# Encoder trunk on one core: order of VectorE's and ScalarE's work around the four retention heads

## The reference

```python
def retention_mixer(h, w_in, w_out, pos):
    q, k, v, g = split(h @ w_in, [D, 2*D, 4*D])          # 4 heads: q, k 256 wide, v, g 512 wide
    q = rotary(q, pos); k = rotary(k, pos) * 256 ** -0.5
    # both directions of the chunked form together give
    o = (q @ k.T * gamma_h ** abs(n - m)) @ v
    o = (o - mean(o)) * rsqrt(var(o) + 1e-6)             # per token and head
    return (silu(g) * o) @ w_out

def rglru_one_direction(x, w_a, b_a, w_i, b_i, lam, reverse):
    r = sigmoid(x @ w_a + b_a); i = sigmoid(x @ w_i + b_i)
    log_a = -8.0 * r * softplus(-lam)                    # softplus(-lam): the "rates", 16 columns here
    a = exp(log_a); u = sqrt(-expm1(2.0 * log_a)) * (i * x)
    return scan(a, u)
```

## Time and profile before

| | before |
|---|---|
| median of 3 runs | 721.08 us (720.83 to 721.31) |
| the profiled execution | 720.02 us, span 718.2 us |
| PE busy, PEld busy | 98%, 82% of the span |
| DVE busy, ACT busy, POOL busy | 85%, 72%, 3% |
| mean granted clock of PE | 0.994 |
| moved by DMA | 134.31 MB, 187 GB/s on average |

### The profile page before, as it was taken

The page is one execution under the profiler, slowest core; times in us unless marked ns, Lnnn a source line. Parts: engine busy times, 40 slices in busy tenths (PEclk is TensorE's granted clock), DMA queues, the critical chain, the costliest instruction groups (busy, mean ns, idle before and its releaser), DMA issues.

```text
span 718.2 us, 15923 instructions
## 1 busy us (share of the span) xinstructions
PE 700.4 (98%) x6495; PEld 586.6 (82%) x6495; DVE 611.4 (85%) x828; ACT 518.5 (72%) x834; POOL 24.4 (3%) x26
## 2 busy tenths in 40 slices
PE   9979999999899999999999999999999999999996
PEld 7858888787699888888888999888888888885464
DVE  6967788887869799998899879999999999999643
ACT  7475673938467688787887688899758889888441
POOL 0001001020010000000000300000000000000000
PEclk9989999999999999999999999999999999999999
DMA  9964634445465165555579961020436656665821
GB/s 343 304 245 134 247 123 144 166 127 213 142 241 205 61 211 201 206 201 175 178 260 407 367 256 60 28 93 1 166 117 195 224 197 215 234 210 208 274 42 59
DMA packets 47323, 134.31 MB, mean 187 GB/s; under 512 B 29728, under 2 KB 30240, under 8 KB 32032
## 3 DMA queue, kind: packets, MB, share of 16 engines
q1 hardware_dynamic: 46976, 133.20, 52.7%
q10 hardware_dynamic: 288, 0.31, 0.1%
HBM read 129.17 MB, written 1.05 MB: 181 GB/s over the span
## 4 chain that ended last, share of the span: by engine, by line
PE 81%; DVE 8%; ACT 6%; SPq 2%; issue 2%; DMA 1%; DVEq 0%; ACTq 0%
PE ps L1638 21%; PE ps L1639 21%; PE ps L1640 21%; PE ps L2075 3%; PE ps L2074 3%; PE ps L2073 3%; SPq L479 2%; DVE w_lo L1006 1%; PE ps L1680 1%; PE ps L1685 1%; PE ps L1681 1%; PE ps L1762 1%; PE ps L1758 1%; PE ps L1759 1%; PE ps L2013 1%
## 5 line engine op out<-in xcount | busy, mean ns | idle before, releaser
L1638 PE MATMUL ps<-a_hi,w_hi 128*128 128x272 f16 (+1 forms) x1000 | 278.2, 278 | 6.2 <-DVE mT L1160 6.2
L1640 PE MATMUL ps<-a_hi,w_lo 128*128 128x272 f16 (+1 forms) x1000 | 278.1, 278 | 0.0
L1639 PE MATMUL ps<-a_lo,w_hi 128*128 128x272 f16 (+1 forms) x1000 | 278.1, 278 | 0.0
L1006 DVE SCALAR_TENSOR_TENSOR w_lo<-stage,w_hi 128x1024 f16<-128x1024 f32 x207 | 248.5, 1229 | 30.7 <-ACT w_hi L548 30.4
L548 ACT ACTIVATE w_hi<-stage 128x1024 f16<-128x1024 f32 x207 | 210.3, 1047 | 51.8 <-PE ps L1640 24.2
L1638 PEld LDWEIGHTS ps<-a_hi,w_hi 128*128 128x128 f16 x1000 | 98.3, 98 | 23.5 <-DVE mT L1160 6.8
L1640 PEld LDWEIGHTS ps<-a_hi,w_lo 128*128 128x128 f16 x1000 | 98.3, 98 | 16.4
L1639 PEld LDWEIGHTS ps<-a_lo,w_hi 128*128 128x128 f16 x1000 | 98.3, 98 | 16.3
L1638 PE MATMUL ps<-y_hi,w_hi 128*128 128x272 f16 (+3 forms) x496 | 106.1, 242 | 0.0
L1639 PE MATMUL ps<-y_lo,w_hi 128*128 128x272 f16 (+3 forms) x496 | 106.1, 242 | 0.0
L1640 PE MATMUL ps<-y_hi,w_lo 128*128 128x272 f16 (+3 forms) x496 | 106.0, 242 | 0.0
(11 more groups left out here) (281 smaller groups left out, 1085.1 us busy)
## 6 DMA issues: line engine op xcount, KB each, us to landing
stage<-in_chunks SPq DMA_DIRECT2D x118, 1024.0 KB
work<-work SPq DMA_DIRECT2D x96, 32.0 KB, 2.0
stage<-in_chunks SPq DMA_DIRECT2D x3, 512.0 KB
decay_all<-in_decay SPq DMA_DIRECT2D x1, 1056.0 KB, 13.6
out<-sq SPq DMA_DIRECT2D x4, 256.0 KB, 2.0
hT<-in_tokens SPq DMA_DIRECT2D x3, 272.0 KB, 6.1
stage<-in_chunks SPq DMA_DIRECT2D x2, 256.0 KB
mT<-in_gains SPq DMA_DIRECT2D x1, 512.0 KB, 6.3
```

The costliest lines, as they stand in the source:

```text
L1006: dve.scalar_tensor_tensor(out=part(1, c, q), in0=flat(stage, c, q), scalar=W_SCALE, in1=part(0, c, q), op0=ALU.mult, op1=ALU.subtract).th ...
L1638: pe.matmul(o, w_h, x_h, start=start, stop=False)
L1639: pe.matmul(o, w_h, x_l, start=False, stop=False)
L1640: return pe.matmul(o, w_l, x_h, start=False, stop=stop)
```

## The change

Three edits, none of which adds or removes an operation. (1) In head 0 DVE evicts the gates and decays the scores ahead of its work on v, which becomes a function `v_halves`; in the other heads the order stays. (2) `lru_rates` is cut in two: the first 13 operations (`lru_series`) run in head 1, ahead of part 0 of chunk c + 3, the last 5 in head 2, behind that part. (3) In the last head the squares (ACT) and their sum and the gating (DVE) move in among the parts of chunk c + 4 = 13: on ACT behind part 1, on DVE behind part 1, with `head_low` of head 2 ahead of part 1.

```diff
--- before.py
+++ after.py
@@ -740,8 +740,11 @@
                 act.activation(gT, gT, ACTF.Silu, scale=-0.5 * UNSCALE).then_inc(g_silu, 1)
                 if h:
                     head_y(h - 1)
-                for q in range(1, SUB):
-                    prep(c + 4, q)
+                prep(c + 4, 1)
+                if h == HEADS - 1:
+                    head_squares(h)
+                prep(c + 4, 2)
+                prep(c + 4, 3)
                 if h == 0:
 
                     act.wait_ge(par_raw, 1)
@@ -749,7 +752,6 @@
                     act.wait_ge(lam_abs, 1)
                     act.activation(lam[:, 1, :], lam[:, 0, :], ACTF.Exp, scale=-1.0).then_inc(lam_exp, 1)
 
-            head_squares(HEADS - 1)
             c = RET_OUT
             estimate(Y, 0, gn_up, HEADS, ESTIMATE[("head", HEADS - 1)])
             head_y(HEADS - 1)
@@ -1205,11 +1207,11 @@
                 dve.tensor_scalar(par[:, LB:LB + 8], par[:, LB:LB + 8], A_SCALE, None,
                                   ALU.mult).then_inc(par_ready, 1)
 
-            def lru_rates():
-
+            t_, z, z2, p_ = lam[:, 1, :], lam[:, 2, :], lam[:, 3, :], lam[:, 4, :]
+
+            def lru_series():
 
                 dve.wait_ge(lam_exp, 1)
-                t_, z, z2, p_ = lam[:, 1, :], lam[:, 2, :], lam[:, 3, :], lam[:, 4, :]
                 link(dve.tensor_scalar(z, t_, 2.0, None, ALU.add))
                 link(dve.reciprocal(z2, z))
                 link(dve.tensor_tensor(z, t_, z2, ALU.mult))
@@ -1218,6 +1220,9 @@
                 for n in range(17, 1, -2):
                     link(dve.scalar_tensor_tensor(out=p_, in0=p_, scalar=1.0 / n, in1=z2, op0=ALU.add,
                                                   op1=ALU.mult))
+
+            def lru_rates():
+
                 link(dve.scalar_tensor_tensor(out=p_, in0=p_, scalar=1.0, in1=z, op0=ALU.add, op1=ALU.mult))
                 link(dve.tensor_scalar(z, par[:, LL:LL + 16], -1.0, 0.0, ALU.mult, ALU.max))
                 link(dve.scalar_tensor_tensor(out=z2, in0=p_, scalar=2.0, in1=z, op0=ALU.mult, op1=ALU.add))
@@ -1248,10 +1253,14 @@
                 if h:
                     head_gated(h - 1)
                 prep(c + 2, 3)
-                for q in range(3 if h else 1):
-                    prep(c + 3, q)
+                if h == 1:
+                    lru_series()
+                prep(c + 3, 0)
                 if h == 2:
                     lru_rates()
+                if h:
+                    prep(c + 3, 1)
+                    prep(c + 3, 2)
 
                 qk = ps[:, A:A + 4, 0:T].rearrange("p (g x) t -> p x g t", x=2)
                 rot = rotq.rearrange("p (g x) t -> p x g t", x=2)
@@ -1265,17 +1274,20 @@
                 for q in range(3 if h else 1, SUB):
                     prep(c + 3, q)
 
-                for n, (_, m) in enumerate(TOK_TILES):
-                    dve.wait_ge(vs_out, NTT * h + n + 1)
-                    dve.tensor_scalar(vsum[0:m, n, 1:2], vsum[0:m, n, 0:1], -1.0 / HEAD_V, None,
-                                      ALU.mult).then_inc(vmean, 1)
-                for n, (_, m) in enumerate(TOK_TILES):
-                    dve.wait_ge(vhi_made, NTT * h + n + 1)
-                    to = v_lo4[0:m, n] if n < 2 else v_hi4[R_LO:R_LO + m, n]
-                    last = dve.scalar_tensor_tensor(out=to, in0=vs[n][0:m], scalar=vsum[0:m, n, 1:2],
-                                                    in1=v_hi4[0:m, n], op0=ALU.add, op1=ALU.subtract)
-                last.then_inc(vlo_made, 1)
-
+                def v_halves():
+                    for n, (_, m) in enumerate(TOK_TILES):
+                        dve.wait_ge(vs_out, NTT * h + n + 1)
+                        dve.tensor_scalar(vsum[0:m, n, 1:2], vsum[0:m, n, 0:1], -1.0 / HEAD_V, None,
+                                          ALU.mult).then_inc(vmean, 1)
+                    for n, (_, m) in enumerate(TOK_TILES):
+                        dve.wait_ge(vhi_made, NTT * h + n + 1)
+                        to = v_lo4[0:m, n] if n < 2 else v_hi4[R_LO:R_LO + m, n]
+                        last = dve.scalar_tensor_tensor(out=to, in0=vs[n][0:m], scalar=vsum[0:m, n, 1:2],
+                                                        in1=v_hi4[0:m, n], op0=ALU.add, op1=ALU.subtract)
+                    last.then_inc(vlo_made, 1)
+
+                if h:
+                    v_halves()
                 dve.wait_ge(w_used, used(c + 2))
                 times_rs(gT, G).then_inc(g_out, 1)
                 dve.wait_ge(s_up, h + 1)
@@ -1285,6 +1297,8 @@
                 last.then_inc(s_dec, 1)
                 if h:
                     rsqrt(rs, A + 3, 0, ESTIMATE[("head", h - 1)])
+                else:
+                    v_halves()
                 dve.wait_ge(shi_made, h + 1)
                 dve.tensor_tensor(s_lo[:, 0:2, :], sT[:, 0:2, :], s_hi[:, 0:2, :], ALU.subtract)
                 dve.tensor_tensor(s_hi[R_HI:R_HI + META, 2, :], sT[0:META, 2, :], s_hi[0:META, 2, :],
@@ -1293,18 +1307,24 @@
                     head_y(h - 1)
                 else:
                     parameters()
-                for q in range(3):
-                    prep(c + 4, q)
+                prep(c + 4, 0)
+                if h + 1 < HEADS:
+                    prep(c + 4, 1)
+                    prep(c + 4, 2)
                 if h:
                     head_low(h - 1)
-                prep(c + 4, 3)
                 if h + 1 < HEADS:
+                    prep(c + 4, 3)
                     v_evict(h + 1)
-
-            dve.wait_ge(o_sq, HEADS)
-            link(dve.tensor_tensor(osq[:, 0:2, :], osq[:, 0:2, :], osq[:, 2:4, :], ALU.add))
-            dve.tensor_tensor(osq[:, 0, :], osq[:, 0, :], osq[:, 1, :], ALU.add).then_inc(sum_o, 1)
-            head_gated(HEADS - 1)
+                else:
+                    prep(c + 4, 1)
+                    dve.wait_ge(o_sq, HEADS)
+                    link(dve.tensor_tensor(osq[:, 0:2, :], osq[:, 0:2, :], osq[:, 2:4, :], ALU.add))
+                    dve.tensor_tensor(osq[:, 0, :], osq[:, 0, :], osq[:, 1, :], ALU.add).then_inc(sum_o, 1)
+                    head_gated(h)
+                    prep(c + 4, 2)
+                    prep(c + 4, 3)
+
             c = RET_OUT
             rsqrt(rs, Y, 0, ESTIMATE[("head", HEADS - 1)])
             head_y(HEADS - 1)
```

## The result

| | before | after |
|---|---|---|
| median | 720.96 us (720.31 to 721.31, 4 runs) | 708.35 us (708.27 to 708.62, 4 runs) |
| the profiled execution | 720.02 us, span 718.2 us | 708.62 us, span 706.8 us |
| mean granted clock of PE | 0.994 | 1.0 |

The ratio is 0.9827, 95% interval 0.981 to 0.9844. The medians are 12.6 us apart. The forecast was 11.4 us and 709.6 us, with a range from 708.5: right in direction, and 0.15 us outside the range at its low end. The two profiled executions are 11.4 us apart, which is the sum of the forecast. Beside the medians 1.2 us are missing; they are in no row of these two traces, and most of what follows looks for them.

What follows compares the result with a forecast made beforehand. PE, busy 98% of the span, was taken as the bound. Savings of 7.37 (head 0), 1.04 (rates) and 3.03 us (last head) sum to 11.44, taking the 721.08 us median to 709.6 us, range 708.5 to 712.3.

Steps and rivals of the forecast that it cites:

- What bounds the kernel: Whole kernel: PE is busy 98% of the span, so only its waits and slow clock can give time.
- the three waits and the slow stretch: PE waits 5.21 us in head 0, 0.97 in head 2, 2.87 in head 3; half clock follows the first.
- Part A: Head 0, gates and score decay ahead of v: chunk 4 starts at 58.50 instead of 65.87, 7.37 us net.
- Part B: Recurrent rates split between heads 1 and 2: head 2's wait goes, 1.04 us gained, no new wait in head 1.
- Part C: Last head, squares, sum and gating earlier: PE's wait for the gating goes, 3.03 us gained; y_lo costs 0.
- The sum: Whole kernel: 11.44 us saved, 708.6 us against the profiled execution, 709.6 us against the median.
- the term of the clock (2.70): Head 0: the slow clock behind the 5.21 us wait costs 2.70 us, all counted as saved.
- rival 1: The low clock stays in head 0 or falls elsewhere after several short pauses: 712.3 us, chance 0.08.
- The range: Whole kernel: 708.5 us (no new wait, spread and profile offset) to 712.3 us.
- 2 (a new wait in head 1): Head 1: v's rows or DVE's transpose come late, PE loses 1 to 2 us: 710.6 to 711.6, chance 0.13.
- 3: Head 0's gates were not held by the v code, so only Part B and Part C count: 717.0 us, chance 0.04.
- 4: Slower than before, v's rows of head 1 landing so late that they hold PE: 723 us, chance 0.02.

Runs made afterwards that it cites:

- run 1: Only head 0's reordering (gates and decay ahead of v) put on the kernel before: 714.25 us, ratio 0.9898.
- run 2: Only the split of the recurrent rates into two halves put on the kernel before: 719.03 us, ratio 0.9977.
- run 4: Kernel before with 40 unread matmuls filling most of head 0's wait for the gates: 718.80 us, ratio 0.996.
- run 7: Kernel before with head 0's reordering and the split rates, last head as before: 713.13 us, ratio 0.9885.
- run 5: Kernel before with 23 zero-weight matmuls filling most of the last head's wait for the gating: 719.66 us, ratio 0.9982.
- run 6: Kernel before with both waits filled, head 0's by 40 matmuls and the last head's by 23: 717.59 us, ratio 0.9954.
- run 9: Changed kernel, but ACT takes the last head's squares behind all its parts, as before; DVE's reordering there stays: 710.14 us, ratio 0.985.
- run 10: Head 0's reordering and split rates on the kernel before, with PE taking the last norm's sum at k = 7 instead of 6: 710.32 us, ratio 0.9855.
- run 12: The changed kernel, unchanged, measured again: 708.33 us, ratio 0.9828 to the kernel before.
- run 11: Changed kernel with v of head 1 transposed ahead of the low part (4,3) instead of behind it: 708.03 us, ratio 0.9823 to the kernel before.

## Why the prediction was right or wrong

**What bounds the kernel** held: the three waits and the slow stretch were the whole of it, and what the heads saved arrived at the end. From the last head's sum to the end of the span it is 718.2 - 185.9 = 532.3 us before and 706.8 - 174.6 = 532.2 after.

**Part A** held in each step, within 0.2 us once the start is taken off. The new wait for v's transpose came nearly as worked out, 0.43 us for 0.6. Net: 65.87 - 43.29 = 22.58 us from the last score matmul to chunk 4 before, 58.63 - 43.60 = 15.03 after, 7.55 for 7.37.

**Part B** held: the 1.04 us came, and the rotation of head 1 is 1.0 us late for the forecast 0.6, hidden as said. DVE's first operation of the series took 0.74 us instead of 0.17, which is most of the difference. It did so in all six profiles with the series in head 1, and 0.17 in head 2 of the kernel before; why was not tried.

**Part C** held for the wait: 3.03 us gone, y_lo of head 3 starts 180.41 - 173.05 = 7.36 us behind the gating, inside the bound of 6.58 + 2.28, and PE did not wait for it.

**The sum** was therefore right for the two executions that were profiled, and wrong for the medians. Its agreement with the profiles to 0.1 us is in part luck: the heads saved 7.55 + 1.04 + 3.03 = 11.6 us, and the changed kernel's profiled execution started 0.3 us later (43.60 for 43.29).

The step that failed is in "What bounds the kernel now": "after the 2.87 us wait the clock was 1.00 (2.4 GHz)". That row was true of one execution and was used for all. Both the term of the clock (2.70) and rival 1, which speaks only of a slow stretch that stays or comes, rest on it; that a second one was there to be saved was not among the cases, so it stood in the sum at nothing. Runs 1, 2, 4 and 7 show 11 to 15 slow matmuls behind that wait, and run 5 that removing them is worth 1.3 us in the medians (0.7 to 1.9 by the interval, which excludes zero). In return head 0's own stretch, taken at 2.70 from one execution, is worth 2.1 to 2.2 in the medians. Run 6 has both at 3.4 us where the sum had 2.70; its interval of 2.4 to 4.3 still holds 2.70, so that difference alone would not decide, and run 5 does.

By the medians the missing 1.2 us is then: 0.7 for the clock (3.4 for 2.70), 0.3 for waits (9.2 from run 6 to the changed kernel, for 8.9 by rows), 0.2 for the new wait in head 0 (0.43 for 0.6). The 0.3 is within the spread, and its place is open. One possible place: before, chunk 3 of head 0 starts when v's rows have landed and been worked on, 7.1 us behind ACT's start on them, and in the seven profiles with that wait, filled or not, it started at 48.35 to 49.45, at 48.78 in the first and at 49.01 in the middle one. In the changed kernel the gates don't hang on this landing.

**The range** failed at its low end for the same reason: with 3.4 for the clock it would have begun at 707.8. It allowed 0.5 us for "spread of runs and of the offset to the profile" while the profile shown was 1.06 us below the median of its own kernel. I moved the sum to the median and took the difference to be the same for the changed kernel. It was 1.06 us before and -0.27 us after: an offset of that size is a cost that some executions have and the profiled one lacked, and an edit can take it away.

**Rivals.** 1 (the slow clock stays or comes): not in the changed kernel, but it is what happened to edits 1 and 2 without edit 3. The Trainium skill's account of small idles (TensorE: Matmul & The Clock Gate, "A second HAM failure mode: psum-queue depth-cycling") is not borne out for waits of 0.3 to 1.5 us here: runs 9, 10 and 12 stayed at 0.998 to 1.0. It speaks of frequent small idles; a single wait of 2.9 us, behind which the clock fell in 4 of 6 profiles, is another case, and my reading of the one row missed it. 2 (a new wait in head 1): no; v's rows were in time, even with the transposes moved in run 11. The latency that the estimate there takes from the Trainium skill (DMA: Bandwidth & Descriptors, "Latency and other measured facts") is given for HBM, and these transfers run from SBUF to SBUF, so it did not bear on them; the landing took 2.1 us for 2.0. 3 and 4: no.

## What to carry to other kernels

When the profile of a kernel is well below its median, list what a longer execution could hold, and treat a clock read behind a wait as one draw: here the same 2.9 us wait cost nothing in one trace and 1.6 us in others, so its removal was worth more than its length. What a stretch is worth in the median is found by filling each wait alone and both together, here 2.2, 1.3 and 3.4 us. Where a wait cannot be removed, shortening it by moving real work ahead of it (one number on PE in run 10) took the slow stretch away as well. Reordering one engine's list pays where its result ends another's wait, and the price is read at the next signal behind what was put back, which here came out to 0.2 us.

## What the runs showed of the hardware

- TensorE's clock falls to the 1.2 GHz level behind a wait of 5.1 to 5.9 us in every profile that has one (5 of 5), for 1.3 to 2.7 us of lost time; behind 2.86 to 2.87 us in 4 of 6 profiles, for about 1.6 us; behind 0.97, 1.29 and 1.47 us in none. What decides between the executions at 2.9 us stays open.
- The length of such a stretch varies from one execution to the next behind nearly the same wait: in head 0 12 to 25 slow matmuls, 1.3 to 2.7 us lost. In medians the two stretches add up: 2.2 us in head 0, 1.3 in the last head, 3.4 together (runs 4 to 6). In single profiles a short one in head 0 came with one in the last head (run 2) and a long one with none (both of before); three profiles don't make a rule, and the clocks of 0.990 to 0.992 speak for executions with both.
- The mean granted clock misses a slow stretch at the start (12 to 26 matmuls about 0.22 us apart where the windows say 1.00) and counts one behind the last matmul that costs nothing (up to 0.002 of the mean).
- Products with zero weights and matmuls that nobody reads kept the clock up as real ones did (run 6, 0.998 to 1.0).
